# A third seven-product pair in the gate/up groups, with its block sums partly added by transfers

## The reference

```python
D_MODEL, SEQ = 2048, 256
D_FF = ((8 * D_MODEL // 3 + 255) // 256) * 256

def _swiglu(x, w_gate, w_up, w_down):
    return (jax.nn.silu(x @ w_gate) * (x @ w_up)) @ w_down

def reference(x, ...):
    x = x + 0.5 * _swiglu(_rmsnorm(x, ffn1_norm[l]), ffn1_w_gate[l], ffn1_w_up[l], ffn1_w_down[l])
    u = _rmsnorm(x, mix_norm[l]) @ w_in[l]
...
    x = x + jnp.concatenate([a_out, b_out], axis=-1) @ w_out[l]
    x = x + 0.5 * _swiglu(_rmsnorm(x, ffn2_norm[l]), ffn2_w_gate[l], ffn2_w_up[l], ffn2_w_down[l])
    return _rmsnorm(x, final_norm[l])
```

## Time and profile before

| | us |
|---|---|
| median of the runs | 1813.52 |
| the profiled execution's time | 1813.86 |
| its span, first to last instruction | 1812.1 |
| TensorE busy with matmuls | 1800.3 |
| VectorE busy | 1412.1 |
| ScalarE busy | 962.1 |
| GpSimd busy | 21.5 |

### The profile page before, as it was taken

One profiled execution on the slowest core, in us unless ns is written; L12 is line 12 of the kernel. 1 busy time (PEld: TensorE's weight loads), 2 busy tenths in 40 slices (PEclk: granted clock), 3 DMA queues, 4 the chain that ended last, 5 costly groups with the idle time before them and its releaser, 6 DMA issues.

```text
span 1812.1 us, 22169 instructions
## 1 busy us (share of the span) xinstructions
PE 1800.3 (99%) x8296; PEld 1500.2 (83%) x8296; DVE 1412.1 (78%) x1665; ACT 962.1 (53%) x1190; POOL 21.5 (1%) x19
## 2 busy tenths in 40 slices
PE   9999999999999999999999999999999999999998
PEld 7888888888888888888888888888888888888887
DVE  7889898889898868666666566889887887678865
ACT  7555445555455546555656445555445555345554
POOL 0000000000000000100000000000000000000000
PEclk9999999999999999999999999999999999999999
DMA  9565655555666657655464466665655557566653
GB/s 334 202 220 201 212 194 192 201 199 199 213 213 225 223 171 245 196 175 169 155 193 162 160 224 223 203 219 197 216 191 193 202 197 258 190 205 224 218 173 114
DMA packets 234115, 367.01 MB, mean 203 GB/s; under 512 B 16560, under 2 KB 95152, under 8 KB 234032
## 3 DMA queue, kind: packets, MB, share of 16 engines
q1 hardware_dynamic: 233120, 364.44, 59.2%
q10 hardware_dynamic: 912, 1.48, 0.2%
HBM read 346.85 MB, written 2.10 MB: 193 GB/s over the span
## 4 chain that ended last, share of the span: by engine, by line
PE 99%; DVE 0%; DMA 0%; issue 0%; ACT 0%; POOL 0%; DVEq 0%; SPq 0%
PE psum L1927 72%; PE psum L1968 14%; PE psum L1840 7%; PE psum L1845 3%; PE psum L1949 1%; PE psum L2117 0%; PE psum L2128 0%; PE psum L2163 0%; PE psum L2143 0%; DVE x_res L1789 0%; DMA w_raw<-in_ffn_gate 0%; PE psum L1807 0%; PE psum L1805 0%; PE psum L1806 0%; PE psum L1899 0%; PE psum L2176 0%
## 5 line engine op out<-in xcount | busy, mean ns | idle before, releaser
L1927 PE MATMUL psum<-w_split,x_split 128*128 128x512 f32 x3792 | 872.9, 390 | 0.0
L1927 PEld LDWEIGHTS psum<-w_split,x_split 128*128 128x128 f32 x3792 | 710.4, 188 | 149.0 <-DVE w_split L1252 1.4
L755 ACT ACTIVATE w_split<-w_raw 128x1024 fp32r<-128x1024 f32 (+1 forms) x520 | 518.6, 1013 | 457.7 <-PE psum L1927 326.7
L1252 DVE TENSOR_TENSOR w_split<-w_raw,w_split 128x1024 fp32r<-128x1024 f32 (+1 forms) x520 | 586.4, 1163 | 95.4 <-ACT w_split L755 89.9
L1927 PE MATMUL psum<-w_split,h_planes 128*128 128x512 f32 x1920 | 439.1, 390 | 0.0
L1927 PEld LDWEIGHTS psum<-w_split,h_planes 128*128 128x128 f32 x1920 | 360.0, 188 | 75.4 <-DVE w_split L1252 1.3
L1102 DVE TENSOR_TENSOR w_split<-w_raw,w_split 128x1024 fp32r<-128x1024 f32 (+1 forms) x244 | 284.0, 1190 | 94.2 <-ACT w_split L645 92.4
L645 ACT ACTIVATE w_split<-w_raw 128x1024 fp32r<-128x1024 f32 (+1 forms) x244 | 247.1, 1032 | 207.2 <-PE psum L1927 158.6
L1968 PE MATMUL psum<-w_split,pair_sums 128*128 128x512 f32 x624 | 162.7, 390 | 0.0
L1968 PEld LDWEIGHTS psum<-w_split,pair_sums 128*128 128x128 f32 x624 | 117.2, 188 | 24.2
L1968 PE MATMUL psum<-w_split,x_split 128*128 128x512 f32 x360 | 94.8, 390 | 0.0
(11 more groups left out here) (240 smaller groups left out, 1046.9 us busy)
## 6 DMA issues: line engine op xcount, KB each, us to landing
w_raw<-in_ffn_up SPq DMA_DIRECT2D x67, 1024.0 KB, 5.4
w_raw<-in_ffn_gate SPq DMA_DIRECT2D x66, 1024.0 KB, 7.9
w_raw<-in_ffn_down SPq DMA_DIRECT2D x64, 1024.0 KB, 5.7
w_raw<-in_w_in SPq DMA_DIRECT2D x48, 512.0 KB, 4.8
w_raw<-in_w_in SPq DMA_DIRECT2D x24, 1024.0 KB, 5.2
w_raw<-in_ffn_gate SPq DMA_DIRECT2D x42, 512.0 KB, 5.5
w_raw<-in_ffn_up SPq DMA_DIRECT2D x40, 512.0 KB, 5.8
w_raw<-in_w_out SPq DMA_DIRECT2D x16, 1024.0 KB, 5.1
```

The lines of the kernel that those rows point to most:

```text
L755: nc.scalar.activation(w_split[:, n % 2, 0, part[0]:part[1]], w_raw[:, slot, part[0]:part[1]], ACT.Copy).then_inc(hi_made, 1)
L1252: nc.vector.tensor_tensor(w_split[:, n % 2, 1, part], w_raw[:, slot, part], w_split[:, n % 2, 0, part].bitcast(F32), ALU.subtract).then_in ...
L1927: ins = mm(psum[:, bank + t, :], x[:, a, t * P:(t + 1) * P], w[:, b, k, :], start=kk == from_ and (a, b) == (0, 0) and t in begins, stop=k ...
```

## The change

The groups of kind `seven_group` get a third pair (k-blocks 10 and 11), so gate quarter 2 and up quarter 2 go; k-blocks 8 and 9 of both sides form one `mixed` job of 24 matmuls. A group has 11 jobs: plain 0, plain 1, blocks 2, mixed 3, blocks 4, blocks 5, plain 6, sums 2, sums 4, sums 5, plain 7.

In groups, the double addition of all three pairs is done by a transfer that GpSimd issues with an add into the raw slot. It reads the two up blocks of the pair from HBM again. VectorE waits for it and does only the two small additions: for the first pair after pass 2, for the second and third after pass 5. `seven_wide` keeps its sums and its order of jobs.

The gate: the copy of bank 4 is in ScalarE's pass 5, one addition (`first_gate`) in VectorE's pass 7, `moved_low` and then the five others in pass 9. SiLU stands in ScalarE's pass 10. From a part's third group on (second, in parts without a plain group) TensorE waits for all six additions of the group before in place of its SiLU. The rows' moves are issued behind raw chunk 6. At the last group ahead of a `seven_wide` the first `pair_of_hidden` is in pass 6, the second, with a `pair_low` ahead of it, in pass 8. Raw slots rotate (`places`). `prepare` and the rope tables' moves stand in the `wide` phase of the first FFN; the plain first group of an FFN builds a third pair of input sums; loops over groups are unrolled.

```diff
-SEVEN_PAIRS = (12, 14)
-SEVEN_JOBS = (("plain", 0), ("plain", 1), ("blocks", 2), ("blocks", 3), ("plain", 4), ("sums", 2), ("sums", 3),
-              ("plain", 5), ("plain", 6), ("plain", 7), ("plain", 8), ("plain", 9))
-SEVEN_FREED_BY = (-4, -3, -2, -1, 0, 1, 5, 6)
+GROUP_PAIRS = (12, 14, 10)
+GROUP_JOBS = (("plain", 0), ("plain", 1), ("blocks", 2), ("mixed", 3), ("blocks", 4), ("blocks", 5), ("plain", 6), ("sums", 2),
+              ("sums", 4), ("sums", 5), ("plain", 7), ("plain", 8), ("plain", 9))
+GROUP_PAIR_OF = {2: 0, 4: 1, 5: 2}
+GROUP_FREED_BY = (-4, -3, -2, -1, 0, 1, 3, 6)
+SUMMED_BY_TRANSFERS = (0, 1, 2)
+GROUP_SUMS_AT = (2, 5, 5)
...
+            def add_blocks(ph, i):
+
+                source = weights_of(ph)
+                for raw, m in GROUP_PAIR_OF.items():
+                    if m not in SUMMED_BY_TRANSFERS:
+                        continue
+                    k = GROUP_PAIRS[m]
+                    blocks = raw_at(ph, i, raw).rearrange("p (q n) -> p q n", n=2 * STRIP)
+                    pool.wait_ge(lo_made, lo_value(seven_base(ph, i) + GROUP_JOBS.index(("blocks", raw))))
+                    nc.gpsimd.dma_start(blocks[:, 0:4:2, :], source(i, 4 + k // 4)[:, k % 4:k % 4 + 2, :],
+                                        accum_op=ALU.add).then_inc(block_sums[m], 16)
...
             def sum_blocks(ph, i, m):
...
+                if by_transfer(ph, m):
+                    dve.wait_ge(block_sums[m], 16 * (group_count(ph, i) + 1))
+                else:
...
+            def first_gate(ph, i):
+
+                dve.wait_ge(chunk_used, used_value(seven_base(ph, i) + 5))
+                dve.wait_ge(first_product, seven_count(ph, i) + 1)
+                nc.vector.tensor_tensor(silu_out[:, 0, :], psum[:, 0, :], silu_out[:, 1, :], ALU.add).then_inc(seven_step, 1)
+
             def seven_gates(ph, i):
 
                 done = seven_steps(ph, i)
-                dve.wait_ge(chunk_used, used_value(seven_base(ph, i) + 6))
-                dve.wait_ge(first_product, seven_count(ph, i) + 1)
-                first = silu_out[:, 0, :]
-                nc.vector.tensor_tensor(seven_up[:, 0, :], psum[:, 6, :], first, ALU.add).then_inc(seven_step, 1)
-                nc.vector.tensor_tensor(first, psum[:, 0, :], first, ALU.add).then_inc(seven_step, 1)
-                dve.wait_ge(seven_step, done + 1)
+                dve.wait_ge(chunk_used, used_value(seven_base(ph, i) + 9))
+                nc.vector.tensor_tensor(seven_up[:, 0, :], psum[:, 6, :], silu_out[:, 1, :], ALU.add).then_inc(seven_step, 1)
+                dve.wait_ge(seven_step, done + 2)
                 nc.vector.tensor_tensor(seven_up[:, 1, :], psum[:, 7, :], seven_up[:, 0, :], ALU.add).then_inc(seven_step, 1)
                 dve.wait_ge(seven_step, done + 3)
+                nc.vector.tensor_tensor(silu_out[:, 1, :], psum[:, 1, :], seven_up[:, 1, :], ALU.add).then_inc(seven_step, 1)
                 nc.vector.tensor_tensor(seven_up[:, 0, :], psum[:, 5, :], seven_up[:, 0, :], ALU.subtract).then_inc(seven_step, 1)
-                nc.vector.tensor_tensor(silu_out[:, 1, :], psum[:, 1, :], seven_up[:, 1, :], ALU.add).then_inc(seven_step, 1)
                 nc.vector.tensor_tensor(seven_up[:, 1, :], psum[:, 5, :], seven_up[:, 1, :], ALU.subtract).then_inc(seven_step, 1)
...
             def seven_group(ph, i, at_end):
-                    if n == 6:
+                    if n == 7:
+                        first_gate(ph, i)
+                    if n == 9:
+                        if not at_first:
+                            moved_low(i - 1, g - 1)
                         seven_gates(ph, i)
-                    if n == 8 and not at_first:
-                        moved_low(i - 1, g - 1)
                     if at_end and ph["h_build"] is not None:
-                        if n == 5:
+                        if n == 6:
                             pair_of_hidden(ph["h_build"], 0, 2)
-                        if n == 7:
+                        if n == 8:
                             pair_low(ph["h_build"], 0, 2)
...
             def seven_group(ph, i):
                 if at_first:
                     pe.wait_ge(psum_freed, s)
+                elif i > ph["plain"]:
+                    pe.wait_ge(seven_step, seven_steps(ph, i))
                 else:
                     pe.wait_ge(silu_done, g)
```

More of the change, by code:

```diff
@@ L82, in hybrid_layer @@
     phases = []
-    s = g = r = part_at = moved_at = extra = sevens = builds = wide_steps = gates = 0
+    s = g = r = part_at = moved_at = extra = sevens = builds = wide_steps = gates = sums = 0
+    group_sums_steps = sum(2 if m in SUMMED_BY_TRANSFERS else 3 for m in range(3))
+    places = [0, 1, 2, 3]
     ff_parts = []
@@ L457, in move_tables, with wide_pair_chunks @@
                                      rope_32[n][0:32, :].rearrange("p (b a d) -> p b a d", a=4, d=32)[:, :, a, :]).then_inc(rope_ready, 16)
+                def wide_pair_chunks(i):
+                    for j in range(8):
+                        sp.wait_ge(lo_made, lo_value(seven_base(ph, i) + (-6 if j == 0 and i else WIDE_FREED_BY[j])))
+                        dst = raw_at(ph, i, j).rearrange("p (k n) -> p k n", n=2 * STRIP)
+                        kind, _ = next(e for e in WIDE_JOBS if e[1] == j)
+                        if kind == "plain":
+                            sp.dma_start(dst, source(2 * i + WIDE_SIDE[j], WIDE_QUARTER[j])).then_inc(landed[j % 4], 16)
+                        else:
+                            for side, done in enumerate((blocks_landed[j - 2], landed[j % 4])):
+                                sp.dma_start(dst[:, 2 * side:2 * side + 2, :],
+                                             source(2 * i + side, 0)[:, 2 * (j - 2):2 * (j - 2) + 2, :]).then_inc(done, 16)
+                        for count in moves.pop(2 * ph["s0"] + 8 * i + j, ()):
+                            move_turned(count)
@@ L459, in seven_chunks @@
                 def seven_chunks(i):
                     for j in range(8):
[L462 to L477, removed]
+                        after_wide = j == 0 and i == 0 and ph["after"]["kind"] == "seven_wide"
@@ L486, in seven_chunks @@
+                        if j == 6 and i:
                             move_turned(ph["moved"] + i)
@@ L608, in norm_rstd, with add_all_blocks @@
                 power(rstd_tok[:, :], mean_sq[:, 0:2], norm_power)
+            def add_blocks(ph, i):
[8 more added lines that the diff above has]
+                                        accum_op=ALU.add).then_inc(block_sums[m], 16)
+            def add_all_blocks(some):
+                for ph in some:
+                    jobs_before["extra"] = ph["extra"]
+                    if ph["kind"] == "ffn_in":
+                        for i in range(ph["plain"], ph["bodies"]):
+                            add_blocks(ph, i)
             norm_rstd(0)
+            mix_at = next(n for n, ph in enumerate(phases) if ph["kind"] == "mix")
+            add_all_blocks(phases[:mix_at])
             norm_rstd(NORM_MIX)
@@ L753, in seven_high @@
                         between()
+                    if kind == "mixed" and used is chunk_used:
+                        act.wait_ge(landed[raw % 4], 16 * (ph["s0"] // 2 + 2 * i + raw // 4 + 1))
                     act.wait_ge(used, used_value(c - 2))
-                    nc.scalar.activation(w_split[:, n % 2, 0, part[0]:part[1]], w_raw[:, slot, part[0]:part[1]], ACT.Copy).then_inc(hi_made, 1)
+                    nc.scalar.activation(w_split[:, split_at(c), 0, part[0]:part[1]], w[:, part[0]:part[1]], ACT.Copy).then_inc(hi_made, 1)
             def seven_group(ph, i, at_end):
@@ L807, in body @@
                             ins.then_inc(silu_done, 1)
-                loop(act, ph["bodies"], body, first=True, last=ph["kn"] != ph["next_kn"] or ph["h_build"] is not None)
+                for i in range(ph["bodies"]):
+                    body(i)
             def seven_wide(ph):
@@ L1253, in seven_low @@
                                             ALU.subtract).then_inc(lo_made, 1)
             def sum_blocks(ph, i, m):
-                b = w_raw[:, 2 + m, :].rearrange("p (q n) -> p q n", n=2 * STRIP)
+                raw = next(r for r, pair in (GROUP_PAIR_OF if in_group(ph) else WIDE_PAIR_OF).items() if pair == m)
+                b = raw_at(ph, i, raw).rearrange("p (q n) -> p q n", n=2 * STRIP)
                 done = weight_sums_value(ph, i, m)
-                dve.wait_ge(lo_made, lo_value(seven_base(ph, i) + 2 + m))
@@ L1394, in body @@
                             fold_sum(0)
-                loop(dve, ph["bodies"], body, first=True, last=True)
+                for i in range(ph["bodies"]):
+                    body(i)
             def seven_wide(ph):
@@ L1931, in wide_chunk, with mixed_chunk @@
                 ins.then_inc(chunk_used, 1)
+            def mixed_chunk(c):
+                w = w_split[:, split_at(c), :, :].rearrange("p l (k n) -> p l k n", n=2 * STRIP)
```

(9 more changed lines are left out.)

320 lines of the change are left out of this document (188 added, 132 removed).

## The result

The changed kernel takes 1859.56 us, median of three runs (1858.98 to 1860.6), against 1813.52: ratio 1.0253, interval 1.023 to 1.0276. The forecast was 1836. The sign was right and the time lies inside the range, but the loss is 46 us where 22.3 were worked out.

What follows compares the result with a forecast made beforehand. TensorE was taken as the bound, with VectorE's chain behind job 9 newly stalling it: -13.6 (matmuls) + 14.7 (gate) + 4.1 + 17.1 (part ends) = +22.3 us, giving 1836 us; range 1815 to 1871.

Steps and rivals of the forecast that it cites:

- What bounds: Whole kernel: TensorE runs groups without a stall worth naming, so removed matmuls pay in full while VectorE keeps ahead.
- the matmuls: In 20 groups: three fewer each, 183 in a group, 41.48 us without stalls; saves 13.6 us.
- The gate behind the groups: At group boundaries: TensorE waits for all six additions, 1.37 us ten times, 0.23 in groups without `moved_low`; costs 14.7 us.
- The chain of 6.8 us: Behind job 9: ScalarE's high part, VectorE's low part, `moved_low` and five additions, with only job 10's 5.44 us as cover.
- everything of it moves by the same amount: Behind the waiting matmul at a group's start: the whole next group shifts by the wait, 1.37 us; period 42.85.
- The ends of parts: Down product waits for SiLU: 4.1 us at three part ends, 17.1 us at three ahead of a `seven_wide`.
- The pair sums: Ahead of a `seven_wide`: input sums in passes 6 and 8 delay VectorE, about 4.2 us passing on to SiLU.
- The clock: Rival: at the three 5.7 us stalls the clock falls to 1.2 GHz, 8.6 us, 1845; within the forecast's shared 0.66.
- The moves: The 16 row moves behind raw chunk 6 delay raw chunk 7, still in time: cost nothing, at worst 1 us a group.
- The sums by transfer: GpSimd's adding transfers in groups: VectorE's work about even, landings covered up to L = 7.57; cost nothing.
- L = 7: Assumed time in us from the low part that releases a transfer to its landing; bounds 5.4 and 11.6.
- The rival of late transfers: Transfers in groups take L of 8 to 10: 1849 us at 8.2, 1871 at 9; chance 0.20.

Runs made afterwards that it cites:

- experiment 2: Changed kernel with the gate's five additions ahead of `moved_low` in VectorE's pass 9: 1841.1 us, 18.5 less than the changed kernel.
- Experiment 3: Changed kernel with both `pair_of_hidden` in passes 0 and 1 of a part's last group instead of 6 and 8: 1846.88 us.
- experiment 1: Changed kernel with all double additions of the block sums back on VectorE, no transfer by GpSimd: 1894.34 us.
- experiment 4: Changed kernel with the `wide` phase's left-over row moves behind raw chunk 5: 1855.49 us; behind raw chunk 6, with `x_from_moved` in pass 6: 1849.69 us.
- experiment 7: The three mends together, but with the double additions on VectorE and no transfer: 1847.05 us.
- the three mends: Changed kernel with gate additions at the start of pass 9, both `pair_of_hidden` in passes 0 and 1, left-over moves behind chunk 6: 1813.19 us, ratio 0.9995.
- experiment 5: Changed kernel with the gate's five additions at the start of VectorE's pass 9, ahead of both low parts and `moved_low`: 1831.13 us.

## Why the prediction was off by half of the loss

What bounds, and the matmuls: right. There are 60 fewer, and a group without a pause is 41.68 where 41.48 was said.

The gate behind the groups: right, to 0.07 us. Forecast 1.37 and 0.25, measured 1.32 and 0.18; 14.7 us forecast, 13.9 measured, and experiment 2 took from each the 1.14 us of the one link that it removed. The chain of 6.8 us was summed from VectorE's start-to-start times in the earlier trace rows, not from the durations of single instructions; that was why it fitted. The period was said to be 42.85 and is 43.3: the step "everything of it moves by the same amount" took a pause at its length. Behind each pause the next 48 matmuls need 0.3 us more, and each group about 0.2 more in any case. These are 3.9 and 4.0 us that the sum has not.

The ends of parts: right as waits. Forecast 5.7 at three places and 1.5, 1.5 and 1.1 at the others; measured 4.75 and 1.49, 1.49 and 1.01: 18.2 in place of 21.2. Experiment 3 confirms that the pair sums are in that chain. The pair sums put 4.75 - 1.49 = 3.3 us into the chain where 4.2 were said: the slack ahead of them was larger than the 0.5 us that I allowed.

The clock: this step failed. It stood among the rivals with 8.6 us and a condition, a fall to 1.2 GHz "for as long again" behind three pauses, and was not in the sum. The clock fell behind all three; what followed them cost 8.3 us, the restarts of 0.3 included, and 2.4 more behind the stall that I had not seen. The mechanism of the rival was right and its size near; what was wrong was to leave it out of the sum. My evidence against it was that pauses up to 1.7 us had left the clock at 1.00. That says nothing of pauses of 5.7, which I was forecasting in the same sum. The right step would have been to put it into the sum as soon as the forecast stalls left the range of the rows. Even below that range it was no sure ground: with the sums on VectorE (experiment 1) the clock fell to 0.50 once behind a pause of 1.79 us.

The moves: this step failed too. "Cost nothing" was worked out for the moves of a steady group, behind raw chunk 6. The same sixteen DMAs also stand, once, behind raw chunk 4 of the first group after the `wide` phase, and there the new order of jobs wants raw chunk 5 two jobs earlier. The trace of before had what was needed: 10.01 us on SyncE's queue, then a load of 5.5 to 7.9 us and the two parts of the weights. In after the moves start at 1643.98 and job 5 is wanted at 1659.54 (1665.91 - 6.37), 15.6 us for 11.1 + 0.7 + 7.75 + 2.4. The stall's price is 8.8 us by the rows (6.37 and 2.4 behind it); experiment 4, which removes it, gained 9.9, of which 1.6 came from the clock elsewhere.

The sums by transfer: right. Taken was L = 7; measured from issue to landing is 6.2 at the median and 8.3 at the longest, and VectorE never waits for one in the profile. The transfers land in 6.2 us beside plain loads of the same size at 5.7 (up) and 4.7 (gate), while VectorE is busy 77% of the time; what the difference is made of, no run shows, but it is covered.

The prediction sets a rule of the Trainium skill against the transfers; it does not bear on them as it was taken to. SBUF — State Buffer, section "SBUF: two separate sides", has a DMA issued by GpSimd held up while VectorE runs an operation in a two-port mode. The same section says, under "Who interferes with whom", that `tensor_tensor` has no such mode, and that a probe saw no stall of a DMA beside it. In a group of after (93.37 to 136.71) 37 of VectorE's 40 instructions are `tensor_tensor`, so by the page VectorE would hold up next to nothing here, and the trace agrees: no transfer was late. The rival of late transfers fell, with its 20 in 100, and experiments 1 and 7 show that the kernel is 34 us slower without them.

Together: forecast 35.9 us of stalls against 39 measured, where 3.8 too much at the gate and the SiLU stood against 6.9 that were missing; nothing forecast for what follows a stall, and 14.6 measured (8.3, 2.4, 3.9); and 4.0 spread over the groups. The time came to lie inside the range because the range reached up to 1871 for late transfers, which did not happen.

## What to carry to other kernels

Where a forecast contains pauses of TensorE, add what follows each: in these runs 0.3 us for a short one, and 1.6 to 3.2 us, half clock included, behind one of 3.6 us or more. When jobs are reordered, walk through each queue in every kind of group, the first and the last above all, and ask of each load which job now wants it. And an edit that removes a stall is worth its size only if the engine that made it has reserve for the next thing it owes: here the three mends won back 46 us and ended level with the kernel before, without the 13.6 that the removed matmuls promised.

## What the runs showed of the hardware

- Behind all 16 pauses of TensorE of 3.6 to 4.8 us (after and experiments 1, 2 and 4) the granted clock fell to the lower level (0.50, 1.2 GHz), and in after was back at 1.00 some 5 us later. Behind the eight of 2.3 to 2.7 us it fell twice (both in experiment 3) and stayed at 1.00 six times (once there, twice in experiment 1, three times in experiment 5). Behind those of 1.3 to 1.6 us it never fell, behind one of the two of 1.79 us in experiment 1 it did (a window of that kernel, from 1.7 us behind the pause):

```profile
1586.30:1588.00 1.70, 1.70 (x5) 1.32 (x5) 1.67 (x3) 0.00 (x0) 0.00 (x0) 0.50 0.02 7
```

- 48 matmuls of 128x512 behind a pause take 11.2 us where the clock stays, 12.8 behind pauses of 2.4 where it falls, 12.5 to 14.1 behind those of 3.6 to 4.8, against 10.9 without a pause.
- A transfer of 512 KB that GpSimd issues with an add onto its target lands in 6.2 us at the median, 0.5 and 1.5 above the plain loads by SyncE of the same size (5.7 and 4.7), and occupies GpSimd for 1.2 us.
- Sixteen moves of 32 KB take SyncE's queue 10.0 us before and 11.1 to 11.2 in the changed kernels, and a load behind them is issued that much later.
